# Retention heads: k and v turned by block transposes and DMAs, and the order of the chunks changed to k, v, q, gate, output

## The reference, cut to what matters

```
proj = h @ w_in
q, k, v, g = split(proj)                  # per head: 256, 256, 512, 512 columns
q = rotary(q, pos) * 256 ** -0.5
k = rotary(k, pos)
scores = einsum('bhld,bhmd->bhlm', q, k) * dmask
out = (einsum('bhlm,bhmv->bhlv', scores, v)
       + einsum('bhld,bhdv->bhlv', q, S) * q_decay[:, :, None])
S_new = S * s_decay[:, None, None] + einsum('bhmd,bhmv->bhdv', k * k_decay[:, :, None], v)
yn = (out - mean(out)) * rsqrt(var(out) + GN_EPS)
return (silu(g) * yn) @ w_out, S_new
```

## Time and profile before

| | |
|---|---|
| median of 3 runs | 1681.27 us (1681.01 to 1682.89) |
| profiled execution | span 1679.0 us from its first to its last instruction; no other time of that execution is given, and the runs' median is 2.3 us above its span |
| eight heads | up to about 1060 us; then convolution, its output and the last norm |
| granted TensorE clock | full in all heads |
| DMA | 325 MB, mean 194 GB/s; 97,047 packets |

### The profile page before, as it was taken

How to read it: one execution, slowest core, us unless ns; L and a number is a source line. 1 busy time by engine, 2 the same in 40 slices (tenths; PEclk the granted TensorE clock), 3 DMA queues, 4 the chain that set the end, 5 groups by cost and what they waited for, 6 DMA issues and landing times.

```text
span 1679.0 us, 30207 instructions
## 1 busy us (share of the span) xinstructions
PE 1660.5 (99%) x11024; PEld 1598.1 (95%) x11024; DVE 1028.6 (61%) x1581; ACT 607.6 (36%) x863; POOL 170.8 (10%) x240
## 2 busy tenths in 40 slices
PE   9999999999999999999999999999999999999996
PEld 9989989989989999998998998999999999999995
DVE  5456556646646636655655664877766666666465
ACT  4333332333333333333333233543333434333333
POOL 1001100100100100100110110420100000000343
PEclk9999999999999999999999999999999999999998
DMA  8447737745854864864774774445754444444442
GB/s 340 152 147 263 265 127 258 281 142 199 302 168 163 283 214 157 288 238 148 263 264 126 260 280 132 138 142 166 256 168 147 142 147 153 138 151 141 150 149 100
DMA packets 97047, 325.25 MB, mean 194 GB/s; under 512 B 13168, under 2 KB 17904, under 8 KB 96960
## 3 DMA queue, kind: packets, MB, share of 16 engines
q1 hardware_dynamic: 76608, 248.71, 44.3%
q0 software_dynamic: 20352, 75.24, 13.2%
HBM read 275.53 MB, written 40.52 MB: 188 GB/s over the span
## 4 chain that ended last, share of the span: by engine, by line
PE 98%; ACT 1%; DVE 0%; DMA 0%; POOL 0%; issue 0%; SPq 0%; ACTq 0%; DVEq 0%; POOLq 0%
PE proj L1262 25%; PE proj L1267 25%; PE proj L1263 25%; PE proj L1422 4%; PE proj L1430 4%; PE proj L1423 4%; PE qs L1385 2%; PE side L1253 1%; PE side L1288 1%; PE side L1246 1%; PE side L1248 1%; PE side L1247 1%; PE qs L1246 0%; PE qs L1247 0%; PE qs L1248 0%; ACT residual L661 0%
## 5 line engine op out<-in xcount | busy, mean ns | idle before, releaser
L1262 PE MATMUL proj<-x_hi,w_hi 128*128 128x322 f32 (+2 forms) x2512 | 766.7, 316 | 0.1
L1263 PE MATMUL proj<-x_lo,w_hi 128*128 128x322 f32 (+2 forms) x2512 | 759.1, 313 | 0.0
L781 DVE TENSOR_TENSOR w_lo<-w_raw,w_hi 128x1024 fp32r<-128x1024 f32 x416 | 513.4, 1237 | 153.8 <-ACT w_hi L530 111.9
L530 ACT CAST w_hi<-w_raw 128x1024 fp32r<-128x1024 f32 x416 | 435.9, 1050 | 454.1 <-PE proj L1263 265.1
L1262 PEld LDWEIGHTS proj<-x_hi,w_hi 128*128 128x128 f32 x2512 | 473.8, 189 | 13.7 <-issue 11.1
L1263 PEld LDWEIGHTS proj<-x_lo,w_hi 128*128 128x128 f32 x2512 | 473.4, 188 | 0.4
L1267 PE MATMUL proj<-x_hi,w_lo 128*128 128x322 f32 (+2 forms) x2512 | 428.8, 313 | 0.3 <-DVE w_lo L781 0.3
L1267 PEld LDWEIGHTS proj<-x_hi,w_lo 128*128 128x128 f32 x2512 | 389.7, 189 | 0.5 <-DVE w_lo L781 0.5
L1422 PE MATMUL proj<-qk_or_z,w_hi 128*128 128x322 f32 x480 | 146.4, 316 | 0.2
L1423 PE MATMUL proj<-qk_or_z,w_hi 128*128 128x322 f32 x480 | 144.0, 311 | 0.0
L810 DVE SCALAR_TENSOR_TENSOR state_update<-state_update,state_decay_of_head,side 128x512 f32<-128x512 f32 x128 | 95.2, 744 | 14.4 <-PE side L1288 11.8
(11 more groups left out here) (207 smaller groups left out, 1303.4 us busy)
## 6 DMA issues: line engine op xcount, KB each, us to landing
w_raw<-w_head SPq DMA_DIRECT2D x256, 512.0 KB, 4.2
w_raw<-w_conv SPq DMA_DIRECT2D x128, 512.0 KB, 3.5
state_update<-s_in POOLq DMA_DIRECT2D x64, 512.0 KB, 7.3
s_out<-state_update POOLq DMA_DIRECT2D x64, 512.0 KB, 5.0
te_for_q_or_prompt_state<-s_in SPq DMA_DIRECT2D x32, 512.0 KB, 9.2
w_raw<-w_cout SPq DMA_DIRECT2D x32, 512.0 KB, 3.5
s_prompt<-te_for_q_or_prompt_state POOLq DMA_DIRECT2D x8, 512.0 KB, 3.6
head_table<-tables POOLq DMA_DIRECT2D x8, 441.0 KB, 5.2
```

The costliest lines, as they stand in the source:

```text
L530: act.copy(w_hi[:, i % SPL, :], w_raw[:, i % RAW, :]).then_inc(w_h.sem, 1)
L781: TT(w_lo[:, i % SPL, :], w_raw[:, i % RAW, :], f(w_hi[:, i % SPL, :]), ALU.subtract).then_inc(w_l.sem, 1)
L1262: mm(bank[:, 0:n], wh[:, k, :], rhs_h(k), start=(first and k == 0), stop=False)
L1263: x = mm(bank[:, 0:n], wh[:, k, :], rhs_l(k), start=False, stop=False)
```

## The change

1. The order of the chunks of a head becomes k (0 to 3), v (4 to 11), q (12 to 15), gate, output; the weights are laid out in that order on the host. k and v stay 336 columns wide, q and gate 322.
2. Neither k nor v is turned by TensorE. VectorE turns 32 x 32 blocks: for k one operation over both blocks of the rotated k, padded from 336 to 352 columns, from SBUF to SBUF; for v one operation per bank straight out of PSUM. DMAs inside SBUF then bring the blocks of each quarter of partitions to their place: 16 for k and 16 for v per head, each 32 partitions x 3 (or 2) pieces of 64 (k) or 128 (v) elements. v's columns are permuted within the head on the host so that its blocks land in order.
3. SP issues these DMAs in groups of four, before loads 9 to 12 (k) and 16 to 19 (v). Before a group it waits for the transposes.
4. The decay of k is no longer a multiplication over the whole k: it is a scale per row when the rows are rounded (ScalarE) and when their low part is made (VectorE, six smaller operations).
5. All scores come behind chunk 17, their masks and roundings to step 18, state times q goes ahead of scores times v behind chunk 18. q's work moves to steps 14 and 16.
6. The plain copies of v on ScalarE go; the last queries use the rows that the DMAs brought. The head's table gets shorter (3 columns of decays instead of 336). POOL's load of the next table also waits for `k_lo`. The stacks of k are issued at loads 14, 15, 20 and 21.

The diff, cut to its core:

```diff
-EARLY = (4, 9)
+EARLY = (4, 16, 17)
-KS_AT = {17: (0, 1, 2), 18: (3, 4, 5), 19: (6, 7), 20: (8, 9), 21: (10, 11)}
+KR_AT = {9: 0, 10: 1, 11: 2, 12: 3}
+VR_AT = {16: 0, 17: 1, 18: 2, 19: 3}
+KS_AT = {14: (0, 1, 2), 15: (3, 4, 5), 20: (6, 7, 8), 21: (9, 10, 11)}
...
+        def rows_in(engine, dst, src, n, sem, b):
+            ms = 3 if b < 3 else 2
+            for a in range(4):
+                engine.dma_start(dst[32 * b:32 * b + 32, 0:ms, n * a:n * a + n],
+                                 src[32 * a:32 * a + 32, b:b + 4 * ms - 3:4, :]).then_inc(sem.sem, 16)
...
             def head_loads(h, first):
                 for i in range(first, CPH):
+                    if i in KR_AT:
+                        sp.wait_ge(k_bt.sem, k_bt.at(h))
+                        rows_in(sp, k_r, k_tr, DKB * 32, kr_in, KR_AT[i])
+                    if i in VR_AT:
+                        sp.wait_ge(p_dve.sem, p_dve.at(h, 6))
+                        rows_in(sp, v_r, v_tr, DVB * 32, vr_in, VR_AT[i])
                     load_chunk(0, h, CPH, i, w_head[h, i])
-                    if i == 17:
-                        sp.wait_ge(kn_l.sem, kn_l.at(h, 3))
+                    if i == 14:
+                        sp.wait_ge(kn_l.sem, kn_l.at(h, 6))
...
                     pool.wait_ge(a_f.sem, a_f.at(h, 3))
+                    pool.wait_ge(kn_l.sem, kn_l.at(h, 6))
...
+                    if i == 9:
+                        act.wait_ge(kr_in.sem, kr_in.at(h, kr_in.per))
+                        act.wait_ge(tab_in.sem, h * 16 + 16)
+                        for m in range(3):
+                            rows = KEY[m][1]
+                            act.activation(by_quarter(k_hi[0:rows, m, :], False), by_quarter(k_r[0:rows, m, :], True), ACT.Identity,
+                                           scale=tab[0:rows, KD_AT + m:KD_AT + m + 1]).then_inc(kn_h.sem, 1)
+                    if i == 17:
+                        act.wait_ge(vr_in.sem, vr_in.at(h, vr_in.per))
+                        for m in range(3):
+                            rows = KEY[m][1]
+                            act.copy(v_hi[0:rows, m, :], v_r[0:rows, m, :]).then_inc(vn_h.sem, 1)
...
                     if i == 4:
                         dve.wait_ge(w_lu.sem, w_lu.at(h, 4))
+                        q_or_k(1, bank_p[1], k_raw, k_t, k_rot, 0)
+                        dve.wait_ge(k_rot.sem, k_rot.at(h, 2))
+                        dve.transpose(k_tr.rearrange("p t (d e) -> p d t e", d=DKB),
+                                      k_pad.rearrange("p d (t e) -> p d t e", e=32)).then_inc(k_bt.sem, 1)
+                    if 6 <= i <= 12 and i % 2 == 0:
+                        d = (i - 6) // 2
+                        dve.wait_ge(w_lu.sem, w_lu.at(h, i))
+                        dve.transpose(v_tr[:, :, 32 * d:32 * d + 32],
+                                      bank_p[d % 2][:, 0:TP].rearrange("p (t e) -> p t e", e=32)).then_inc(p_dve.sem, 1)
+                    if i == 9:
+                        dve.wait_ge(tab_in.sem, h * 16 + 16)
+                        for m in range(3):
+                            dve.wait_ge(kn_h.sem, kn_h.at(h, m + 1))
+                            for d in range(DKB):
...
-                        dec = tab[:, KD_AT:KD_AT + T].unsqueeze(1).to_broadcast([P, DKB, T])
-                        TT(k_dec, k_raw, dec, ALU.mult).then_inc(k_d.sem, 1)
...
-                                x = turn(bank[0:rows, c0 + P * d:c0 + P * d + P], k_dec[:, d, t0:t0 + rows])
-                    if i in (11, 13):
+                    if i == 17:
                         pe.wait_ge(q_l.sem, q_l.at(h))
                         pe.wait_ge(k_l.sem, k_l.at(h))
-                        for m in ((0, 1), (2,))[(i - 11) // 2]:
+                        pe.wait_ge(s_new.sem, s_new.at(h, 0))
+                        for m in range(3):
...
-                                x = turn(bank_r[m][0:rows, P * d:P * d + P], v_t[:, d, t0:t0 + rows])
...
-                    g, kept = i // 2, i < 4 or i >= 16
+                    g, kept = i // 2, i >= 12
```

More of the change, by code:

```diff
@@ L56 @@
 KD_AT = QD_AT + NSAMP
-TAB = KD_AT + T
+TAB = KD_AT + len(KEY)
+TP = 352
+TB = TP // 32
 HALF = 1024
@@ L61 @@
 FIRST_W = {0: 1, 5: 2, 7: 3}
-SCALE_AT = (15, 16, 21, 22)
+SCALE_AT = (7, 9, 21, 22)
 CPH = 32
@@ L596, in side @@
+                    if 18 <= i <= 24 and i % 2 == 0:
+                        g = 8 + (i - 18) // 2
+                        act.wait_ge(w_lu.sem, w_lu.at(h, 2 * g + 2))
+                        act.wait_ge(sc_done.sem, sc_done.at(h, 3))
+                        act.activation(gate[:, g - 8, :], bank_p[g % 2][:, 0:N], ACT.Silu).then_inc(p_act.sem, 1)
+                    if i == 18:
+                        for m in range(3):
                             act.wait_ge(a_f.sem, a_f.at(h, m + 1))
@@ L600, in side @@
                             act.copy(a_hi[0:rows, A_AT[m]:A_AT[m] + n], at[0:rows]).then_inc(a_h.sem, 1)
[L601 to L612, removed]
                     if i == 19:
@@ L787, in _ @@
             dve.memset(y_f[:, 0, :].bitcast(F32), 0.0).then_inc(warm_set.sem, 1)
+            for e in range(2):
+                dve.memset(bank_p[e][:, T:TP], 0.0).then_inc(pad_set.sem, 1)
             for c in range(XC):
@@ L798, in _ @@
             dve.wait_ge(zero_set.sem, 1)
+            dve.wait_ge(pad_set.sem, 2)
             add = ALU.add
@@ L895, in side @@
                         TT(q_lo, q_raw, f(q_hi), ALU.subtract).then_inc(q_l.sem, 1)
[L896 to L905, removed]
-                        dec = tab[:, KD_AT:KD_AT + T].unsqueeze(1).to_broadcast([P, DKB, T])
-                        TT(k_dec, k_raw, dec, ALU.mult).then_inc(k_d.sem, 1)
-                    if i == 12:
+                    if i == 17:
                         for m in range(3):
                             rows = KEY[m][1]
[L911 to L917, removed]
+                            dve.wait_ge(vn_h.sem, vn_h.at(h, m + 1))
+                            TT(v_lo[0:rows, m, :], v_r[0:rows, m, :], f(v_hi[0:rows, m, :]), ALU.subtract).then_inc(vn_l.sem, 1)
+                    for ms in ((0, 1), (2,)) if i == 18 else ():
                         for m in ms:
@@ L933, in side @@
                             TT(a_lo[0:rows, at], tmp[0:rows, m % 2, 0:n], f(a_hi[0:rows, at]), ALU.subtract).then_inc(a_l.sem, 1)
[L934 to L938, removed]
                     if i == 19:
@@ L1272, in _ @@
             pe.wait_ge(warm_set.sem, 1)
+            pe.wait_ge(pad_set.sem, 2)
             zeros = y_f[:, 0, :]
@@ L1314, in side @@
                         pe.wait_ge(fold_set.sem, 1)
[L1315 to L1322, removed]
-                                x = turn(bank[0:rows, c0 + P * d:c0 + P * d + P], k_dec[:, d, t0:t0 + rows])
-                            x.then_inc(kt_done.sem, 1)
-                    if i in (11, 13):
+                    if i == 17:
                         pe.wait_ge(q_l.sem, q_l.at(h))
                         pe.wait_ge(k_l.sem, k_l.at(h))
-                        for m in ((0, 1), (2,))[(i - 11) // 2]:
+                        pe.wait_ge(s_new.sem, s_new.at(h, 0))
+                        for m in range(3):
                             (t0, rows), (c0, n), bank = KEY[m], SC[m], bank_r[(1, 2, 0)[m]]
@@ L1337, in side @@
                             x.then_inc(sc_done.sem, 1)
[L1338 to L1342, removed]
-                                x = turn(bank_r[m][0:rows, P * d:P * d + P], v_t[:, d, t0:t0 + rows])
-                            x.then_inc(vt_done.sem, 1)
-                    if i == 18:
-                        pe.wait_ge(vn_l.sem, vn_l.at(h, 3))
-                        pe.wait_ge(a_l.sem, a_l.at(h, 3))
-                        for t in range(2):
-                            rows = QRY[t][1]
-                            for m in range(t + 1):
-                                at = A_AT[m] + QRY[t][0] - SC[m][0]
-                                x = three(bank_r[t][0:rows, :], a_hi[:, at:at + rows], a_lo[:, at:at + rows],
-                                          v_hi[:, m, :], v_lo[:, m, :], m == 0, m == t)
-                            x.then_inc(y_done.sem, 1)
                     if i == 23:
@@ L1387, in side @@
                         pe.wait_ge(aq_set.sem, aq_set.at(h, 2))
-                        pe.wait_ge(vq_set.sem, vq_set.at(h, 2))
+                        pe.wait_ge(vr_in.sem, vr_in.at(h, vr_in.per))
                         for m in range(2):
-                            x = mm(bank_q[group[m], :], aq[:, m, :], vq[:, m, :], start=False, stop=True)
+                            x = mm(bank_q[group[m], :], aq[:, m, :], v_r[:, m, :], start=False, stop=True)
                         x.then_inc(s_q.sem, 1)
+                    if i == 18:
+                        pe.wait_ge(vn_l.sem, vn_l.at(h, 3))
+                        pe.wait_ge(a_l.sem, a_l.at(h, 3))
+                        for t in range(2):
+                            rows = QRY[t][1]
```

(18 more changed lines are left out.)

80 lines of the change are left out of this document (43 added, 37 removed).

## The result

The changed kernel takes 1664.44 us (median of 4, 1664.02 to 1666.28), the kernel before 1681.19 (4 runs): a ratio of 0.990, interval 0.9886 to 0.9914, faster by 16.75 us. Forecast were 1665.1 us and 16.2 us less. The profiled execution of after took 1664.84 us, its span is 1663.3, 15.7 less than that of before.

What follows compares the result with a forecast made beforehand. TensorE, busy 99% and 98% of the chain, was taken as the bound: 15.6 us for the transposes plus 0.6 for hand-overs, all else hidden, made 16.2 us less than 1681.27, so 1665.1 us; range 1662 to 1673.

Steps and rivals of the forecast that it cites:

- The rival of 39 us by durations: On TensorE, all heads: the whole duration of 144 transposes comes back, 39 us, giving 1642 us; chance 0.02.
- Hand-over, at most 0.6: TensorE, scores together behind chunk 17: one hand-over to the projection fewer per head, 0.6 us gained, bounds 0 and 0.8.
- VectorE in chunk 4: k's block transpose takes 0.9 us, hidden up to 2.6 us; priced like the reciprocal 4.7 us, costing 17 us.
- SP's issue, 0.57: On SP, 32 more DMAs per head at 0.57 us per issue: 2.3 us per group of four, less than a chunk.
- Landing and the first deadline: k's rows land 3.8 us after issue, 16.7 us after chunk 3; needed by 20.5 for chunk 10, margin 3.8 us.
- B: The prediction's time mark in each head: the end of chunk 3, where VectorE's rotation starts.
- the rival of SP's issue: SP's issue becomes the wait: k's rows late from 0.81 us per issue, up to 98 us more, 1779; chance 0.08.
- k's rows land late: Rival: landing takes 9.2 us, rows 1.6 us late before chunk 10, 13 us of gain lost, 1678 us; chance 0.11.
- The second deadline: v's rows, for chunk 18: in 14.8 us after chunk 11, felt by TensorE after 22; load 16 has 6 us spare.
- C: The prediction's time mark in each head: the end of chunk 11, just before SP waits for the last transposed v block.
- the DMA engines become the bound: Rival, where v's groups meet full DMA engines: load 16 loses over 5 us; 2 us stall per head gives 1681; chance 0.05.
- ScalarE's wait for k's rows: Sign against the prediction: ScalarE waiting for the k or v rows by DMA for over 5 us.

## Why the prediction was right, step by step

- **TensorE bounds, and the transposes are worth 15.6 us.** Right. Per head 1.95 forecast, 1.94 by putting them back and 1.93 by taking them out of before. The rival of 39 us by durations is excluded.
- **Hand-over, at most 0.6.** A little small: 0.13 us per head, 1.0 in all, over its bound of 0.8. What in the rest of the change gives it was not taken apart.
- **VectorE in chunk 4.** Right: the transpose took 0.91 us. Chunk 5's residual ended at 292.78 and TensorE came to it at 294.32: 1.5 us to spare, where 2.6 - 0.9 = 1.7 was forecast. The upper bound, priced like the reciprocal, lay far off. v's transpose took 0.55 (0.5), k's low parts 0.35 (0.3).
- **SP's issue, 0.57.** It is 0.60; the longest was 1.63. The rival would have begun at 0.81. That its mechanism is real is shown by the runs with six issues for k and eight for v: slower than before by 2.3% and by 1.4 to 1.7%. Its price was too low: it counts the wait alone, and with six issues for k 35.1 us of waits became 51.3 us of span.
- **Landing and the first deadline.** The end held, the step did not. The rows came at B + 19.7 in place of B + 16.7, and the margin was 0.8 us in place of 3.8. The last group ended 303.67 - 288.31 = 15.4 us behind B, 2.4 later than the sum of issues had it: the four groups took 10.6 us where 16 x 0.57 = 9.1 stood, and the gaps between groups and loads, not counted, 0.9. The landing took 4.4 us for 3.8. With 0.8 us over 16 issues the rival of SP's issue would have begun at about 0.65 us per issue, not at 0.81, and the rival "k's rows land late" was nearer than its 0.11 says. That the end held was luck as far as this sum goes: it was off by 3.0 us of a margin of 3.8. The groups of k also move 352 KB per head, not 88 in all.
- **The second deadline.** Load 16 was to land by C + 8 (C is 318.5 in head 3) and was cast at C + 11.9, with the DMA engines full; its high part was made 1.3 us before TensorE came to it, at C + 14.2. ScalarE got v's rows at C + 20.5 without waiting, and TensorE would have felt them behind C + 22. Of the rivals, "the DMA engines become the bound" is the one that took something, 0.6 us in one head.
- **The sum.** 8 x 2.06 = 16.5, less 0.6 in head 3 is 15.9; the spans differ by 15.7. The forecast was 16.2; the medians differ by 16.75, and the runs of one kernel spread by 2 us. The median of after lies 1.1 us above the profiled span, not 2.3.
- **One sign was badly chosen.** ScalarE's wait for k's rows, 24.3 us, is over the 5 us that were to show the prediction wrong, and costs nothing: ScalarE is busy 36%. The sign that counts is TensorE's wait.

TensorE's listed waits come to 3.6 us in the whole of after, 2.9 of them in the first 9 us, and leaving the copies out gains nothing that can be seen; a further gain would have to come out of TensorE's own matmuls again.

## What to carry to other kernels

Where TensorE is busy 99% and the whole chain, price work taken from it by the distance between its neighbours with and without it, not by its duration (1.94 us per head, not 4.9). Then count issues on the queue that carries the replacement: DMAs of 0.6 us each between loads that are due every 3.6 us leave room for four, not for eight; six held for v's rows and not for k's. And check the slack with a dose of the suspected cost; a margin of 0.8 us looks the same in the time as one of 8.

## What was not expected of the hardware

- **A stall costs more than its wait.** Behind a stall of 4.9 us TensorE's granted clock was 0.50 for most of the next chunk: 2.4 us on top of the wait. Seven of the eight stalls of that run had such a stretch behind them.
- **Full DMA engines at 219 GB/s.** With pieces of 512 bytes among the weights the share stayed at 1.05 to 1.10 while the rate fell from 401 to 219 GB/s. A full share alone does not show such pieces: in before it was 1.05 at 262 GB/s from 313.6 to 317.4, where 32 of 275 packets are under 2 KB.
- **A later issue that lands no later.** With the engines full, a load issued 2.2 to 3.8 us later in its head was cast 0.1 us earlier in the mean of seven heads.
